# Casts per feature tile at the feed-forward entries, and alternating partition halves in a linear attention's small matmuls

## The reference

```python
def rmsnorm(x, g, eps=1e-6):
    y = x * lax.rsqrt(jnp.mean(x * x, axis=-1, keepdims=True) + eps)
    return y * g

x = x + mixer(...) @ w_out                 # phase "mix" (first block), "pw2" (its second layer), "mix2"
h = rmsnorm(x, ffn_norm)                   # the three feed-forward entries
x = x + (jax.nn.silu(h @ w_gate) * (h @ w_up)) @ w_down

# linear attention, per head: S_t = diag(a_t) S_(t-1) + k_t^T v_t,  o_t = q_t S_t, in chunks of 64 tokens
scores = jnp.einsum('bhtd,bhsd,bhtsd->bhts', qc, kc, decay)
o = jnp.einsum('bhts,bhsv->bhtv', scores, vc) + jnp.einsum('bhtd,bhdv->bhtv', qc * jnp.exp(bcum), state)
```

## Time and profile before

| | us |
|---|---|
| median of 3 runs | 1923.76 |
| lowest, highest | 1920.2, 1928.8 |
| profiled execution | 1923.76 |
| its span | 1922.0 |
| mean granted TensorE clock | 0.976 |
| TensorE busy | 1855.8 (97%) |
| VectorE busy | 1058.1 (55%) |
| ScalarE busy | 713.9 (37%) |
| GpSimd busy | 222.3 (12%) |

### The profile page before, as it was taken

How to read it: one execution, slowest core, us unless ns; L and a number is a source line. 1 busy time by engine, 2 the same in 40 slices (tenths; PEclk the granted TensorE clock), 3 DMA queues, 4 the chain that set the end, 5 groups by cost and what they waited for, 6 DMA issues and landing times.

```text
span 1922.0 us, 22962 instructions
## 1 busy us (share of the span) xinstructions
PE 1855.8 (97%) x8651; PEld 1537.6 (80%) x8651; DVE 1058.1 (55%) x1295; ACT 713.9 (37%) x804; POOL 222.3 (12%) x137
## 2 busy tenths in 40 slices
PE   7898999999999999999999999999999999999997
PEld 5787877888888788877888888888887788888876
DVE  7647645444444587765444444477755444444455
ACT  4316534343433312244344333332223443433342
POOL 1600000000000467600000000022610000000000
PEclk9879999999999999999999999999999999999998
DMA  4310023333233321122333323332213333333332
GB/s 160 110 50 1 32 79 88 109 88 107 69 91 105 93 61 44 45 75 79 101 96 87 95 77 104 97 93 66 66 45 88 88 87 109 87 89 101 91 97 71
DMA packets 280028, 159.51 MB, mean 83 GB/s; under 512 B 7776, under 2 KB 278016, under 8 KB 279968
## 3 DMA queue, kind: packets, MB, share of 16 engines
q1 hardware_dynamic: 278912, 155.44, 28.2%
q0 software_dynamic: 624, 1.67, 0.3%
q10 hardware_dynamic: 432, 1.57, 0.2%
HBM read 156.56 MB, written 2.10 MB: 83 GB/s over the span
## 4 chain that ended last, share of the span: by engine, by line
PE 93%; DVE 4%; ACT 1%; issue 1%; DMA 0%; POOL 0%; DVEq 0%; SPq 0%; ACTq 0%
PE ps L794 29%; PE ps L796 28%; PE ps L795 28%; PE ps L981 2%; PE ps L1171 1%; PE ps L966 1%; PE ps L943 1%; DVE wlo L1278 1%; DVE rstd L1320 1%; DMA raw<-in_nsa_w_in_dram 0%; DVE act_lo L1308 0%; PE ps L1198 0%; DVE acc L1387 0%; PE ps L854 0%; DVE acc L1377 0%
## 5 line engine op out<-in xcount | busy, mean ns | idle before, releaser
L794 PE MATMUL ps<-act_hi,whi 128*128 128x512 f32 x1764 | 701.6, 398 | 38.4 <-DVE act_lo L1310 22.9
L795 PE MATMUL ps<-act_lo,whi 128*128 128x512 f32 x1764 | 694.7, 394 | 0.0
L796 PE MATMUL ps<-act_hi,wlo 128*128 128x512 f32 x1764 | 694.6, 394 | 0.0
L1278 DVE TENSOR_TENSOR wlo<-raw,whi 128x2048 fp32r<-128x2048 f32 (+1 forms) x157 | 360.8, 2298 | 218.1 <-ACT whi L497 217.0
L794 PEld LDWEIGHTS ps<-act_hi,whi 128*128 128x128 f32 x1764 | 336.6, 191 | 117.5 <-issue 32.4
L795 PEld LDWEIGHTS ps<-act_lo,whi 128*128 128x128 f32 x1764 | 336.4, 191 | 71.1 <-issue 1.2
L796 PEld LDWEIGHTS ps<-act_hi,wlo 128*128 128x128 f32 x1764 | 336.0, 190 | 71.4
L497 ACT ACTIVATE whi<-raw 128x2048 fp32r<-128x2048 f32 (+1 forms) x165 | 310.3, 1881 | 202.4 <-PE ps L796 201.9
L1292 DVE TENSOR_TENSOR t<-ps,rstd 128x512 f32<-128x512 f32 (+1 forms) x151 | 103.6, 688 | 233.2 <-PE ps L796 232.9
L794 PE MATMUL ps<-hid_hi,whi 128*128 128x512 f32 x528 | 208.0, 394 | 0.0
L796 PE MATMUL ps<-hid_hi,wlo 128*128 128x512 f32 x528 | 207.0, 392 | 0.0
(11 more groups left out here) (343 smaller groups left out, 1613.1 us busy)
## 6 DMA issues: line engine op xcount, KB each, us to landing
raw<-in_ffn_w_gate_dram SPq DMA_DIRECT2D x44, 512.0 KB, 3.9
raw<-in_ffn_w_up_dram SPq DMA_DIRECT2D x44, 512.0 KB, 5.1
raw<-in_w_gate_upffn_dram SPq DMA_DIRECT2D x44, 512.0 KB, 4.8
raw<-in_ffn_w_down_dram SPq DMA_DIRECT2D x32, 384.0 KB, 3.1
raw<-in_conv_w_pw_dram SPq DMA_DIRECT2D x24, 512.0 KB, 4.3
raw<-in_w_in_dram SPq DMA_DIRECT2D x24, 512.0 KB, 4.6
raw<-in_ffn_w_down_dram SPq DMA_DIRECT2D x32, 320.0 KB, 3.6
raw<-in_nsa_w_in_dram SPq DMA_DIRECT2D x14, 512.0 KB, 4.7
```

Of the source, the lines that this page charges most:

```text
L794: pe.matmul(out, lhs[0], rhs[0], start=start, stop=False)
L795: pe.matmul(out, lhs[0], rhs[1], start=False, stop=False)
L796: return pe.matmul(out, lhs[1], rhs[0], start=False, stop=stop)
L1278: ve.tensor_tensor(wlo[:, n % 2, a], raw[:, n % 2, a], whi[:, n % 2, a].bitcast(F32), ALU.subtract)\
```

## The change

At the three feed-forward entries the last panel before them is written out (`last_panel`): in the last tile every group of three matmuls counts `act_free`, and ScalarE casts feature tiles 0 to 6 each behind its own count, before it deals with output tile 7. Tile 7 is cast after the panel, ahead of its square. VectorE makes the low parts of tiles 0 to 5 after the square of tile 6, and those of 6 and 7 after it has added output tile 7. The first up panel is done by `first_panel`: the two tiles take turns, feature tile by feature tile, and the sum of squares stands after the fifth feature tile. High part and split of the second up panel come before the root and the reciprocal; in the loop they move from the start of a round to the end of the one before, and the last round is written out. The convolution entry gets the same interleaved first panel, and nothing else of this.

In the linear attention the matmuls of levels, self scores and the state part of the outputs alternate between the lower and the upper half. `self_scores` and `add_self` now take one feature tile per call, with both halves, a bank for each half; the outputs go by pairs of heads: eight full-height matmuls, then seven pairs of 64-partition ones.

```diff
             def late(q, name, use, ahead=0):
...
                     for k in (2 * i, 2 * i + 1):
+                        if k == KD - 1:
+                            for kk in range(KD - 1):
+                                act.wait_ge(sem("act_free"), 7 * use + kk + 1)
+                                cast(act_hi[:, kk], x[:, kk], f"xhi{q}", gain(q, kk))
                         act.wait_ge(bank_free, T0[name] + k + 5)
+                        if k == KD - 1:
+                            act.wait_ge(panel_done, N0[name] + 4)
+                            cast(act_hi[:, k], x[:, k], f"xhi{q}", gain(q, k))
                         square(q, k, x[:, k])
-                act.wait_ge(panel_done, N0[name] + 4)
-                for k in range(KD):
-                    cast(act_hi[:, k], x[:, k], f"xhi{q}", gain(q, k))
...
             def ffn(f, q, up_, dn, qn):
+                hi(N0[up_] + 1)
                 root(q)
...
+                    act.wait_ge(sem("hidden_set"), 2 * i + (KF * f + j + 1))
+                    cast(hid_hi[:, bass.ds(2 * i + j, 1), :], t1[:, j], "hidden_hi")
+                    if more:
+                        hi(N0[up_] + j + 2, i)
...
-            def first_panel(name, act_wait):
+            def first_panel(name, act_wait, mid=None):
...
                 for k in range(KD):
+                    if mid and k == 5:
+                        mid()
                     pe.wait_ge(sem(act_wait), k + 1)
                     for c in range(2):
                         ins = mm3(bank(T + c)[:, :], slot(n, k, 256, c * P), act_k(k), k == 0, k == KD - 1)
...
+            def last_panel(name):
+
+                n, T = N0[name] + 3, T0[name] + 6
+                pe.wait_ge(split_done, n + 1)
+                tile(T, 0, lambda k: slot(n, k), act_k, range(KD), tile_done)
+                pe.wait_ge(bank_free, T + 2)
+                for k in range(KD):
+                    mm3(bank(T + 1)[:, :], slot(n, k, 256, P), act_k(k), k == 0, k == KD - 1)\
+                        .then_inc(sem("act_free") if k < KD - 1 else panel_done, 1)
...
-                panel2(up_, 0, act_wait=f"act{q}", after=lambda: sumsq(q))
+                first_panel(up_, f"act{q}", lambda: sumsq(q))
...
-            panel2("pw1", 0, act_wait=f"act{CONVIN}", after=lambda: sumsq(CONVIN))
+            first_panel("pw1", f"act{CONVIN}", lambda: sumsq(CONVIN))
...
-                for h in (0, 2, 1, 3):
-                    part, c, a = head(h)
+                for c in range(2):
                     for w in range(TB):
                         o = c * S + w * P
...
+                        for half in range(2):
+                            part = head(half)[0]
+                            right = qd[part, o:o + P].rearrange("p (b t) -> p b t", t=2 * m)[:, :, m:]
+                            out = ps[6 + half][:, (c * TB + w) * CH:(c * TB + w + 1) * CH]
+                            ins = pe.matmul(out, kd[part, o:o + P], right, start=True, stop=True)
...
                     for ch in range(1, NCH):
                         o = c * S + ch * CH
...
+                        for h in (2 * c, 2 * c + 1):
+                            part = head(h)[0]
+                            ins = pe.matmul(ps[4 + h][:, ch * CH:(ch + 1) * CH], state[part, c, ch, :],
+                                            qe[part, o:o + CH], start=False, stop=ch == NCH - 1,
+                                            skip_group_check=True)
...
+                        if k == KD - 1:
+                            low_norm(q, k - 1)
+                            low_norm(q, k)
                         add_square(q, k)
-                for k in range(KD):
-                    low_norm(q, k)
+                        if k == KD - 2:
+                            for kk in range(KD - 2):
+                                low_norm(q, kk)
...
             def ffn(f, q, up_, dn, qn):
+                lo(N0[up_] + 1)
                 inv(q)
```

More of the change, by code:

```diff
@@ L616, in _, with late @@
                 cast(act_hi[:, k], ps[4 + k][:, :], "o_hi")
-            def late(q, name, ahead=0):
+            def late(q, name, use, ahead=0):
                 for i in range(4):
@@ L762, in _ @@
                 cast(act_hi[:, h], t1[:, h % 2], "go_hi")
-            late(FFN3, "mix2")
+            late(FFN3, "mix2", 2)
             ffn(2, FFN3, "up3", "dn3", PLE)
@@ L1024, in _ @@
             panel2("mix", 1)
-            with pe.Fori(1, 2) as i:
-                for j in range(2):
-                    panel2("mix", j, i)
+            panel2("mix", 0, 1)
+            last_panel("mix")
             def ffn(f, q, up_, dn):
-                panel2(up_, 0, act_wait=f"act{q}", after=lambda: sumsq(q))
+                first_panel(up_, f"act{q}", lambda: sumsq(q))
                 panel2(up_, 1)
@@ L1101, in _ @@
             panel2("pw2", 1)
-            with pe.Fori(1, 2) as i:
-                for j in range(2):
-                    panel2("pw2", j, i)
+            panel2("pw2", 0, 1)
+            last_panel("pw2")
             ffn(1, FFN2, "up2", "dn2")
@@ L1164, in level @@
                     pe.wait_ge(sem("lev_added"), 2 * lev)
-                for h in (0, 2, 1, 3):
-                    part, c, a = head(h)
+                for c in range(2):
                     for w in range(TB):
                         o = c * S + w * P
[L1169 to L1173, removed]
+                        for half in range(2):
+                            part = head(half)[0]
+                            right = qd[part, o:o + P].rearrange("p (b t) -> p b t", t=2 * m)[:, :, m:]
+                            out = ps[6 + half][:, (c * TB + w) * CH:(c * TB + w + 1) * CH]
+                            ins = pe.matmul(out, kd[part, o:o + P], right, start=True, stop=True)
+                            if c == 1 and w == TB - 1:
+                                ins.then_inc(sem("lev_scores"), 1)
             def updates(chunks):
@@ L1244, in _ @@
             panel2("mix2", 1)
-            with pe.Fori(1, 2) as i:
-                for j in range(2):
-                    panel2("mix2", j, i)
+            panel2("mix2", 0, 1)
+            last_panel("mix2")
             ffn(2, FFN3, "up3", "dn3")
@@ L1595, in _, with hidden @@
             late(FFN1, "mix")
             def ffn(f, q, up_, dn, qn):
+                lo(N0[up_] + 1)
                 inv(q)
-                with ve.Fori(0, KF // 2) as i:
-                    for j in range(2):
[L1601 to L1610, removed]
+                def hidden(i, j, more):
+                    scaled(t1[:, j], first(up_, j, i))
+                    scaled(t2[:, j], second(up_, j, i))
+                    ve.wait_ge(sem("silu_ready"), 2 * i + (KF * f + j + 1))
+                    ve.wait_ge(bank_free, 4 * i + (T0[up_] + 2 * j + 6))
+                    ve.tensor_tensor(t1[:, j], t2[:, j], t3[:, j], ALU.mult).then_inc(sem("hidden_set"), 1)
+                    k = bass.ds(2 * i + j, 1)
+                    ve.wait_ge(sem("hidden_hi"), 2 * i + (KF * f + j + 1))
+                    ve.tensor_tensor(hid_lo[:, k, :], t1[:, j], hid_hi[:, k, :].bitcast(F32), ALU.subtract)\
+                        .then_inc(sem("hidden_lo"), 1)
+                    if more:
+                        lo(N0[up_] + j + 2, i)
@@ L1611, in ffn @@
+                with ve.Fori(0, KF // 2 - 1) as i:
+                    for j in range(2):
+                        hidden(i, j, True)
+                hidden(KF // 2 - 1, 0, True)
+                hidden(KF // 2 - 1, 1, False)
                 if qn == FINAL:
```

58 lines of the change are left out of this document (30 added, 28 removed).

## The result

The changed kernel takes 1893.57 us (median of 4 runs, 1892.44 to 1894.71) against 1925.33 for the kernel before on the same chip: ratio 0.9837, 95% interval 0.9813 to 0.9862, 1.6% faster. The profiled execution took 1892.44, 31.3 us less than the one before. The forecast was 1888.0, the range 1881 to 1898.

A forecast was written before the change was run, and what follows sets the result against it. TensorE, busy 97% of the span, was taken as the bound. Gains of 19.5 us at the entries and 17.8 in the linear attention, less 1.4 at the convolution entry, made 35.9: 1923.76 to 1887.9 us, range 1881 to 1898.

The forecast's parts named there:

- Entries: Three feed-forward entries: early casts and early second split remove 6.5 us of idleness, low clock and waiting each; gain 19.5 us.
- the third panel's split: Feed-forward entries: next late item in VectorE's queue, done near 25 and needed at 28, 3 us of slack.
- Convolution entry: Entry to the convolution: the sum moves later, delaying root and GpSimd's split; loss 1.4 us, at best 0.
- Alternating halves: Linear attention matmuls: two halves run at once, a level 1.94 instead of 3.32 us, outputs 7.4 instead of 11.2.
- Rivals 2 and 5: Linear attention: halves don't overlap, 1905.7, chance 0.05; each change of half empties the array, 1930.5, chance 0.02.
- The 5.8 for levels 0 to 2: Linear attention, levels 0 to 2: 4.1 us from shorter levels and 1.7 from the clock after level 0.
- The two steps: Steps with self scores, levels 3 and 4: VectorE bounds at 15.1 us each, gain 5.1; TensorE waits 2.5 before level 5.
- Level 5: Level 5 and last ccx panel: 1.4 us from the shorter level and 1.7 from the clock, gain 3.1.
- rival 1: Clock falls all the same after three entries and levels 0 and 5, five times 1.7 us: 1896, chance 0.12.
- Rival 3: Steps with self scores: VectorE and GpSimd take turns, so the two steps gain nothing: 1893, chance 0.05.
- The price of 20.5: Rival 3's step length: GpSimd's 12.1 us plus VectorE's 8.4 of two-SBUF-input work, more than the 17.9 measured.

The follow-up runs named there:

- casts_late: Changed kernel with the casts of the three feed-forward entries after the whole panel again; 1904.32 us, one execution.
- split_late: Changed kernel with VectorE's split of the second up panel behind the reciprocal again at the three entries; 1908.22 us, one execution.
- no_short_conv: Changed kernel with two of three taps of GpSimd's short convolution left out of the computation; 1887.97 us, one execution.
- conv_later: Changed kernel with tile-by-tile first panels, ScalarE's convolution-entry casts before the root, and GpSimd's second short convolution held until level 5's operands are made; 1878.48 us.
- entries_only: Changed kernel with levels, self scores and outputs of the linear attention in the order of before; 1909.11 us, ratio 0.9926 to the kernel before.
- no_interleave: Changed kernel with first panels tile by tile again at all four entries, sum after the first tile; 1889.43 us, ratio 0.9824 to the kernel before.
- gla_only: Kernel before with only the linear attention's matmuls alternating between halves; 1908.54 us, ratio 0.9920.

## Why the prediction was right

**Entries.** Forecast 19.5, measured 20.0. Mechanism and slack held: 2.9 of idleness, 1.8 of clock and 1.8 behind the reciprocal went, no wait for the third panel's split came. `casts_late` and `split_late` show the pieces singly; the clock's share is the least certain of them, since it did not fall behind every such wait. VectorE's queue followed the forecast within 0.3 us: the second panel's split ended 12.2 us after the last tile began (12.5 forecast).

**Convolution entry.** Forecast a loss of 1.4, measured 1.3; the path (sum, root, high part, GpSimd's split) was the one named. What the step missed is the clock: another 2.8 us at half behind it, which I had left in no term.

**Alternating halves.** Forecast 1.94 a level and 7.4 for the outputs, measured 1.93 and 7.3. That fp32 records, which come in pairs on the same half, overlap as the others do was an inference from the state updates, and it held. Rivals 2 and 5 are out: no price per alternation shows. The 5.8 for levels 0 to 2 with the clock behind level 0 was 5.7.

**The two steps, the term that was mis-sized.** I took VectorE's 15.1 us a step from the kernel before and said that GpSimd's lengthening was "already in" it. It took 16.1: the gain was 2.9 in place of 5.1. In the shorter step GpSimd's distance computation moved onto the product of the keys, which went from 1.21 to 2.91, while that of the queries fell to 1.71; the two together explain 1.9 of the 2.2 us that the term was too large. A busy time that holds another engine's interference is no constant of the work; it belongs to the old alignment. `no_short_conv` and `conv_later` show that the excess is GpSimd's. TensorE waited 4.1 us in all, 1.2 before level 4 and 2.9 before level 5, where I had forecast 2.5 before level 5 alone.

**Level 5.** Forecast 3.1, measured 1.4: the clock fell behind it all the same, which was rival 1 for one of its five places. That there would be a wait was forecast, but not that it would bring the clock down. All eight kernels with alternating halves in which TensorE waited around level 5 show the clock at half behind it; in `no_short_conv` and `conv_later`, without the wait, it stayed full.

**Rival 3** had the mechanism right and its price wrong (the steps did shrink), and my ground against it was false. "The trace disagrees, since both engines' busy times overlap" doesn't follow, because an instruction that is held up counts as busy. The last section shows the two engines taking turns. The price of 20.5 counted such waits as work: GpSimd's 12.1 us of a step add up to 8.9 at the shortest length that each of its instructions has in the kernel before, its distances for instance at 1.89 and `t<-t` at 1.28 in place of 1.62.

Together: terms too large by 2.2, 1.7 and 2.8, too small by 0.5, 1.3 us less ahead of the first entry and 0.3 elsewhere, where nothing was changed: 4.6, for the 4.5 us between 1887.9 and 1892.44. The misses on the large side sum to 6.7 us; that the total came so near owes 1.6 us to luck, in code that the change doesn't touch.

## What to carry to other kernels

Where an operand buffer is reused, let the consumer count its passes per tile instead of per panel, and look behind the first gap at once for what the same queue makes late next: at these entries either half of the change alone would have left 3 to 5 us standing. Alternating the two halves took the fp32 matmuls on 64 partitions from 3.32 to 1.93 us in a level and to half in the outputs; the relief lands on whoever drains and feeds them, so price that engine with its disturbances laid out anew, not with its old busy time. Don't carry a pattern to a place without the problem: the interleaved panel at the convolution entry only moved the sum, and with it the path that mattered there.

## What the runs showed of the hardware

**VectorE and GpSimd.** GpSimd's instruction began at 1332.39 and ended at 1335.15; the product began at 1333.31 and ended at 1336.22, 1.07 later, 0.14 less than the 1.21 that it takes alone. More rows of the changed kernel, first VectorE, then GpSimd:

```profile
1324.01 0.69 DVE L1851 TENSOR_TENSOR at<-at,t 128x512 f32<-128x512 f32 x1
1324.73 0.69 DVE L1833 TENSOR_TENSOR t<-ps,glm 128x512 f32<-128x512 f32 x1
1325.46 0.94 DVE L1839 TENSOR_TENSOR at<-at,t 128x512 f32<-128x512 f32 x1
1327.89 3.27 DVE L1306 TENSOR_TENSOR wlo<-raw,whi 128x2048 fp32r<-128x2048 f32 x1
```

```profile
1324.22 1.63 POOL L470 TENSOR_TENSOR t<-t 128x512 f32<-128x512 f32 x1
1327.38 1.63 POOL L470 TENSOR_TENSOR t<-t 128x512 f32<-128x512 f32 x1
```

The addition at 1325.46 ends 0.55 after GpSimd's 1325.85 (0.69 alone), the split at 1327.89 ends 2.15 after GpSimd's 1329.01 (2.29 alone). The other way round, GpSimd's instruction at 1324.22 began beside the addition at 1324.01 and ends 1.15 after it (1.28 alone). The Trainium skill, "SBUF — State Buffer", section "SBUF: two separate sides", says that such a pair takes turns, and "the other fully blocks". The trace agrees, and not for this pair alone: between 1270 and 1372 us there are 24 additions to `at`, products of the operands and splits that began while an instruction of GpSimd was running, with 0.07 to 1.93 us of it left, and they all ended 0.55 to 0.56 (additions), 1.08 to 1.09 (products) and 2.15 to 2.21 us (splits) after its end, not after their own usual time. VectorE's instructions that read PSUM (`t<-ps,glm` at 1324.73) keep their 0.69 beside GpSimd. So two overlapping busy times are no sign that both engines work, and a busy time taken beside the other engine is not the work's own.

**The clock.** In the kernel before it fell behind four of the six levels of 3.3 us (0, 3, 4 and 5; not behind 1 and 2). In `entries_only`, whose linear attention is the same code, it fell behind levels 0 to 3 and not behind 4 and 5. With levels of 1.9 it fell in this part only where TensorE had also waited, and not each time: of seven kernels with the wait of 1.2 before level 4 it fell behind that one in `no_interleave` alone. Of nine waits of 2.9 for low halves at the feed-forward entries (the kernel before, `gla_only`, `casts_late`) eight brought it down, of the three waits of 2.9 for the split in `split_late` one. The wait of 2.0 us at the convolution entry cost 1.7 of clock besides. In the layer norm 150 us later the clock stayed low for 6.8, 13.7 or 17.1 us with the same code. What decides in these cases isn't shown.
